# The gate tiles and the first output projection of the merge put between the pieces of a scan

## What is computed

```python
def mixing_sublayer(u_lat, u_ctx, ...):
    a_lat, b_lat, gates_lat = jnp.split(u_lat @ w_in, split_at, axis=-1)
    oa_lat, _ = run_a(a_lat, state_a)              # gated delta rule, "the first mixer"
    ob_lat, _ = run_b(to_col_major(b_lat, rows), state_b)   # RWKV-7 scan, "the second mixer"
    ob_lat = to_row_major(ob_lat, rows)
    g_a, g_b = jnp.split(gates_lat, 2, axis=-1)
    y = jax.nn.sigmoid(g_a) * (oa_lat @ w_o_a) + jax.nn.sigmoid(g_b) * (ob_lat @ w_o_b)
    return y @ w_out
```

## Time and profile before

| | |
|---|---|
| median of 3 runs | 2622.01 us (2617.77 to 2626.14) |
| the profiled execution: its time | 2621.55 us |
| its span | 2619.7 us |
| PE busy | 2470.2 us, 94% |
| DVE, ACT, POOL busy | 1424.4 us (54%), 1186.0 us (45%), 306.8 us (12%) |
| mean granted clock of PE | 0.97 |
| the head of the scan, the scan and the merge | 1881.97 to 2259.1 us |

### The profile page before, as it was taken

The page is one execution under the profiler, slowest core; times in us unless marked ns, Lnnn a source line. Parts: engine busy times, 40 slices in busy tenths (PEclk is TensorE's granted clock), DMA queues, the critical chain, the costliest instruction groups (busy, mean ns, idle before and its releaser), DMA issues.

```text
span 2619.7 us, 52357 instructions
## 1 busy us (share of the span) xinstructions
PE 2470.2 (94%) x23199; PEld 2135.1 (82%) x23199; DVE 1424.4 (54%) x2229; ACT 1186.0 (45%) x1707; POOL 306.8 (12%) x425
## 2 busy tenths in 40 slices
PE   6999999999999999999999989899888889799998
PEld 6999888799999998878899965785477778678786
DVE  4654545466546645443666456445245540278885
ACT  4434466444444444564444355321254421167773
POOL 0100000021101100000311000641133321000000
PEclk8999999999999999999999989889899899899999
DMA  6754522256656644322566411101100004379993
GB/s 217 246 192 167 192 97 104 81 195 233 216 178 213 230 164 171 129 97 101 173 237 222 154 66 46 54 15 57 65 4 4 4 27 141 96 240 365 365 365 126
DMA packets 268884, 396.07 MB, mean 151 GB/s; under 512 B 9320, under 2 KB 172829, under 8 KB 268525
## 3 DMA queue, kind: packets, MB, share of 16 engines
q1 hardware_dynamic: 266921, 389.25, 43.4%
q0 software_dynamic: 1120, 2.17, 0.3%
q10 hardware_dynamic: 612, 1.24, 0.1%
HBM read 391.59 MB, written 1.05 MB: 150 GB/s over the span
## 4 chain that ended last, share of the span: by engine, by line
PE 75%; DVE 8%; issue 5%; DMA 5%; ACT 4%; POOL 2%; SPq 0%; ACTq 0%; DVEq 0%; POOLq 0%
PE ps L282 74%; DMA RB<-in_moe_w_up 5%; DVE gwl L431 2%; POOL H L1415 2%; ACT gwh L422 1%; POOL AR L2535 0%; ACT wh L422 0%; PE ps L1093 0%; DVE wl L431 0%; PE ps L520 0%; DVE AR L1677 0%; ACT AR L2752 0%; DMA RB<-in_ffn_w_gu 0%; ACT AR L2744 0%; DVE AT L1178 0%
## 5 line engine op out<-in xcount | busy, mean ns | idle before, releaser
L431 DVE TENSOR_TENSOR wl<-RB,wh 128x2048 fp32r<-128x2048 f32 (+4 forms) x188 | 412.5, 2197 | 294.5 <-ACT wh L422 293.9
L282 PE MATMUL ps<-H,RB 128*128 128x256 f32 (+1 forms) x1712 | 455.5, 423 | 1.1 <-ACT H L1515 1.1
L422 ACT ACTIVATE wh<-RB 128x2048 fp32r<-128x2048 f32 (+4 forms) x188 | 342.3, 1825 | 236.7 <-PE ps L282 205.3
L282 PEld LDWEIGHTS ps<-H,RB 128*128 128x128 f32 x1712 | 325.5, 193 | 115.1 <-issue 77.4
L282 PE MATMUL ps<-xhf,wl 128*128 128x256 f32 x1408 | 404.4, 287 | 14.0 <-DVE xlf L651 9.3
L282 PE MATMUL ps<-xlf,wh 128*128 128x256 f32 x1408 | 401.0, 285 | 0.0
L282 PE MATMUL ps<-xhf,wh 128*128 128x256 f32 x1408 | 400.8, 285 | 0.0
L282 PE MATMUL ps<-AR 64*64 64x64 f32 (+4 forms) x8296 | 276.1, 242 | 47.2 <-issue 19.7
L282 PEld LDWEIGHTS ps<-AR 64*64 64x64 f32 (+2 forms) x8296 | 241.9, 148 | 80.3 <-issue 51.0
L282 PEld LDWEIGHTS ps<-xhf,wl 128*128 128x128 f32 x1408 | 273.0, 194 | 24.9 <-DVE wl L431 14.8
L282 PEld LDWEIGHTS ps<-xlf,wh 128*128 128x128 f32 x1408 | 273.0, 194 | 0.1
(11 more groups left out here) (425 smaller groups left out, 4155.0 us busy)
## 6 DMA issues: line engine op xcount, KB each, us to landing
RB<-in_ffn_w_gu SPq DMA_DIRECT2D x88, 1024.0 KB, 7.7
RB<-in_w_in SPq DMA_DIRECT2D x25, 2048.0 KB, 7.7
RB<-in_ffn_w_down SPq DMA_DIRECT2D x16, 2048.0 KB, 7.8
RB<-in_w_gate SPq DMA_DIRECT2D x16, 2048.0 KB, 8.2
RB<-in_moe_w_gate SPq DMA_DIRECT2D x32, 1024.0 KB, 7.7
RB<-in_moe_w_up SPq DMA_DIRECT2D x32, 1024.0 KB, 10.2
RB<-in_moe_w_down SPq DMA_DIRECT2D x32, 1024.0 KB, 8.2
RB<-in_ada_w SPq DMA_DIRECT2D x12, 2048.0 KB, 9.9
```

What stands on the lines that cost most here:

```text
L282: return M.matmul(o, lhsT, rhs, start=start, stop=stop, skip_group_check=True)
L422: S.activation(self.pair(h)[0], of(slot_of(*key)), ACT.Copy).then_inc(*did("high", *mark))
L431: V.tensor_tensor(lo, of(slot_of(*key)), hi.bitcast(F32), ALU.subtract).then_inc(*did("low", *mark))
```

## The change

1. The first mixer's 8 output tiles (`merge0`), its 8 gate tiles (`gate0`) and the second mixer's first 4 gate tiles (`gate1`) move into `rwkv_order`, so that all engines meet them between pieces of the scan. In the head stand two output tiles and one gate tile; slots -1 to 3 have one output tile each ahead of `mid` 4 and one gate tile each at their end; slots -1 and 3 have one more gate tile ahead of `mid` 2 (slot 3 with an output tile); slots 4 and 5 end on a `gate1`, and slot 7 has two.
2. POOL's product of a gate tile (now L2960) stands at the same place of POOL's order, and its result goes to other memory (Y0).
3. The meetings ahead of the scan and of the merge go; single waits take their place. The small matrices are copied two tiles earlier in the shift, and the last low-rank sigmoid moves behind the rate's piece of unit 0.
4. `base_b` stands ahead of `prep` 0 in each slot, so that ACT's copies for the inverse come ahead of the decay's sigmoid.
5. The remaining merge starts with the last 4 gate tiles. DVE now reads the second mixer's output tile from PSUM, multiplies and adds it; ACT's copy and POOL's product of it go. The loads of lnx by POOL are issued as soon as the scan's last masks are out. The weights' jobs follow the new order.

The core of the diff:

```diff
-        for i, n in enumerate(("w_o_a_2", "w_o_b_2")):
-            job(("o", i), fill_k(A[n][0], 0, 4, 0, DM), ("merge", i, 7))
+        job(("o", 0), fill_k(A["w_o_a_2"][0], 0, 4, 0, DM), ("merge", 0, 7))
+        for i in range(2):
             for u in range(2):
                 job(("mgate", i, u), fill_k(w2in, 0, KD, G_0 + 1024 * i + 512 * u, 512), ("mgate", i, 4 * u + 3))
+        job(("o", 1), fill_k(A["w_o_b_2"][0], 0, 4, 0, DM), ("merge", 1, 7))
...
-            order = prepared(0, *range(7)) + [(("products", 0, o),) for o in range(2)]
+            def fill(*pieces):
+                return [(piece,) for piece in pieces]
+
+            def gate(c):
+                return [("gate0", c, 0), ("gate0", c, 1)]
+
+            order = prepared(0, 0, 1) + fill(("merge0", 0, 0)) + prepared(0, 2) + fill(*gate(0), ("merge0", 1, 0))
+            order += prepared(0, *range(3, 7)) + [(("products", 0, o),) for o in range(2)]
+            sigmoid = {-1: gate(1), 3: [("merge0", 6, 0)] + gate(6)}
+            middle = {i: [("merge0", i + 3, 0)] for i in range(-1, 3)}
+            middle[3] = [("merge0", 7, 0)]
+            end = {i: gate(i + 3) for i in range(-1, 3)}
+            end[3] = gate(7)
+            end.update({4: [("gate1", 0, 0)], 5: [("gate1", 1, 0)]})
 ...
-                slot = [solve(n, "base_a", 0)] + prepared(p, 0) + [solve(n, "base_b", 0)]
+                slot = [solve(n, "base_a", 0), solve(n, "base_b", 0)] + prepared(p, 0)
                 slot += [solve(n, "mid", 1) + out(i, "out_s", 0), unit(i, "solved", 0), solve(n, "more", 1)]
-                slot += prepared(p, 1)
+                slot += prepared(p, 1) + fill(*sigmoid.get(i, ()))
                 slot += [solve(n, "mid", 2) + unit(i, "state", 0)] + prepared(p, 2) + [solve(n, "more", 2)]
                 slot += [unit(i, "early", 1) + out(i, "out", 0)] + prepared(p, 3)
+                slot += fill(("gate1", 2, 0)) if i == 7 else []
                 slot += [solve(n, "mid", 3) + unit(n, "rows", 0), unit(i, "solved", 1)] + prepared(p, 4)
-                slot += [solve(n, "more", 3)] + prepared(p, 5, 6)
+                slot += [solve(n, "more", 3)] + prepared(p, 5, 6) + fill(*middle.get(i, ()))
+                slot += fill(("gate1", 3, 0)) if i == 7 else []
                 slot += [solve(n, "mid", 4) + out(i, "out_s", 1), solve(n, "more", 4)]
                 slot += [unit(n, "early", 0) + unit(i, "state", 1), solve(n, "mid", 5) + out(i, "out", 1)]
-                slot += [unit(p, "products", 0), unit(p, "products", 1), solve(n, "more", 5)]
+                slot += [unit(p, "products", 0), unit(p, "products", 1), solve(n, "more", 5)] + fill(*end.get(i, ()))
...
+                    if n == 14:
+
+                        AC.wait_ge(*upto("low_rank"))
+                        AC.wait_ge(*at("shift", 13))
+                        S.activation(W2, EARLY[0], ACT.Copy).then_inc(*did("w2"))
...
+                    if n == 13:
+                        DV.wait_ge(*upto("low_rank"))
+                        DV.wait_ge(*at("shift", 13))
+                        V.tensor_copy(A2, EARLY[1])
+                        for i in range(2):
+                            ins = V.tensor_copy(W0[i], EARLY[3][64 * i:64 * i + 1, :])
+                        ins.then_inc(*did("a2"))
...
-            everyone(("moved", 14), ("low_act", 14), ("rv_rows", 3), ("unit_kk", 3))
-
-
-            AC.wait_ge(*upto("low_rank"))
-            S.activation(W2, EARLY[0], ACT.Copy).then_inc(*did("w2"))
-            PO.wait_ge(*upto("low_rank"))
-            P.tensor_copy(G2, EARLY[2]).then_inc(*did("g2"))
-            DV.wait_ge(*upto("low_rank"))
-            V.tensor_copy(A2, EARLY[1])
-            for i in range(2):
-                ins = V.tensor_copy(W0[i], EARLY[3][64 * i:64 * i + 1, :])
-            ins.then_inc(*did("a2"))
-            for mark in (("w2",), ("g2",), ("a2",)):
-                PE.wait_ge(*at(*mark))
...
+                if what == "merge0":
+                    sv = slot_of("o", 0).rearrange("p (k n) -> p k n", k=4)
+                    PE.wait_ge(*landed("o", 0))
+                    PE.wait_ge(*at("o_rows", 1))
+                    ps = bank(("merge", 0, i), ("yb", 0, i), among=kept if i > 1 else (3, 4))
+                    for k in range(4):
+                        ins = mm(ps[:, 0:T], sv[:, k, 128 * i:128 * i + 128], OAT[:, k, :], k == 0, k == 3)
+                    ins.then_inc(*did("merge", 0, i))
+                elif what == "gate0":
+                    sv = slot_of("mgate", 0, i // 4).rearrange("p (k n) -> p k n", k=KD)
+                    if x == 0:
+                        PE.wait_ge(*landed("mgate", 0, i // 4))
+                        bank(("mgate", 0, i), ("mgated", 0, i), among=kept if i else (3, 4))
+                    ps = ps_of("mgate", 0, i)
+                    for k in range(4 * x, 4 * x + 4):
+                        ins = mm(ps[:, 0:T], sv[:, k, 128 * (i % 4):128 * (i % 4) + 128], HA[:, k, :], k == 0, k == KD - 1)
+                    if x:
+                        ins.then_inc(*did("mgate", 0, i))
+                elif what == "gate1":
+                    gate1_pe(i, others)
+                elif what == "prep" and x == 0:
+                    for mark in (("low_act", 12), ("w2",), ("a2",)):
+                        PE.wait_ge(*at(*mark))
...
+                    if what == "merge0":
+                        AC.wait_ge(*at("merge", 0, i))
+                        if i > 1:
+                            AC.wait_ge(*at("weighed_b", 0, i - 2))
+                        S.activation(YBR[i % 2], ps_of("merge", 0, i)[:, 0:T], ACT.Copy).then_inc(*did("yb", 0, i))
+                    elif what == "gate0" and x:
+                        AC.wait_ge(*at("mgate", 0, i))
+                        if i > 1:
+                            AC.wait_ge(*at("weighed_b", 0, i - 2))
+                        S.activation(SGB[i % 2], ps_of("mgate", 0, i)[:, 0:T], ACT.Sigmoid).then_inc(*did("mgated", 0, i))
+                    elif what == "gate1":
+                        gate1_act(i)
...
-                    if what == "prep" and x == 3:
+                    if what == "gate0" and x:
+                        PO.wait_ge(*at("mgated", 0, i))
+                        if i > 3:
+                            PO.wait_ge(*at("kt", 3))
+                        P.tensor_tensor(Y0[i], YBR[i % 2], SGB[i % 2], ALU.mult).then_inc(*did("weighed_b", 0, i))
+                    elif what == "prep" and x == 3:
+                        PO.wait_ge(*at("unit_kk", 3))
                         if i > 1:
...
+                for c in range(4, KD):
+                    gate1_pe(c, every_bank)
+                PE.wait_ge(*at("low_act", 14))
+                PE.wait_ge(*at("g2"))
...
+                    DV.wait_ge(*at("merge", 1, c))
+                    DV.wait_ge(*at("mgated", 1, c))
+                    V.tensor_tensor(SG1[c], ps_of("merge", 1, c)[:, 0:T], SG1[c], ALU.mult).then_inc(*did("yb_v", c))
+                    DV.wait_ge(*at("yb_v", c))
+                    V.tensor_tensor(Y0[c], Y0[c], SG1[c], ALU.add).then_inc(*did("summed", c))
...
+                PO.wait_ge(*at("kt", 7))
+                PO.wait_ge(*at("bon_in", 7))
...
-                for i in range(2):
-                    for c in range(KD):
-                        PO.wait_ge(*at("mgated", i, c))
-                        P.tensor_tensor(YB[i][:, c, :], YB[i][:, c, :], SGB[:, c % 4, :], ALU.mult).then_inc(
-                            *did("weighed_b", i, c))
 
```

More of the change, by code:

```diff
@@ L1452, in block2 @@
             rwkv(area, *tail)
-            merge(area)
         class LastHead:
@@ L2489, in shift_dve @@
                 ins.then_inc(*did("blk"))
-                for n in range(16):
+                for n in range(15):
                     tail_dve(n)
                     i, j = divmod(n, 4)
+                    if n == 13:
[5 more added lines that the diff above has]
+                        ins.then_inc(*did("a2"))
+                        i = 3
                     if 5 <= n < 9:
@@ L2601, in pairs_pe @@
                 u = units[i]
-                if what == "prep" and x == 0:
+                if what == "merge0":
[21 more added lines that the diff above has]
+                        PE.wait_ge(*at(*mark))
                     ps = bank(("w_in", i), ("w_sig", i), among=others)
@@ L2727, in pairs_pe, with gate1_pe, gate1_act @@
                         yield
+            def gate1_pe(c, banks):
+                sv = slot_of("mgate", 1, c // 4).rearrange("p (k n) -> p k n", k=KD)
+                PE.wait_ge(*landed("mgate", 1, c // 4))
+                ps = bank(("mgate", 1, c), ("mgated", 1, c), among=banks)
+                for k in range(KD):
+                    ins = mm(ps[:, 0:T], sv[:, k, 128 * (c % 4):128 * (c % 4) + 128], HA[:, k, :], k == 0, k == KD - 1)
+                ins.then_inc(*did("mgate", 1, c))
+            def gate1_act(c):
+                AC.wait_ge(*at("mgate", 1, c))
```

(14 more changed lines are left out.)

79 lines of the change are left out of this document (33 added, 46 removed).

## The result

The changed kernel takes 2641.16 us (median of 15 runs, 2626.23 to 2651.92), the kernel before, run beside it, 2619.83 us (median of 15, 2610.25 to 2626.14). The ratio is 1.0074 with a 95% interval from 1.0053 to 1.0094 (it isn't the quotient of the two medians, which is 1.0081): **slower by 0.74%, some 19 us**. The forecast was 2626. The result sits at the top of the range, where the second rival stood (the clock falls for long, 2642).

What follows compares the result with a forecast made beforehand. PE holds 75% of the chain of waits; the merge is solid matmuls, the scan has holes. Seven terms were summed to -4.1 us, the clock's +10 made +6, trimmed to +4.5: 2626 us, range 2604 to 2642.

Steps and rivals of the forecast that it cites:

- the second rival: Scan: clock falls last 8 to 10 us, each costing 4.5, so the change is slower: +20.5, 2642 us; chance 0.25.
- The merge: Merge after the scan: output and gate tiles moved out, and the meeting's hole gone, take off 55.7 us, leaving 62.
- The ends of slots: Ends of slots -1 to 3: five gate tiles, each with a 2.55 us PE standstill behind POOL's product and mask: +26.3 us.
- `gate1` at the ends of slots 4 and 5: Two gate tiles without POOL product, 3.47 us each less holes of 1.53 and 0.92: +4.5 us.
- The gates ahead of level 2: Slots -1 and 3: level 2's masks wait behind POOL's product, +5.8 and +9.1, together +14.9 us.
- The head: Between shift and first level of slot -1: PE goes on at full speed, -3.9 us, bounds 0 and -7.
- The output tiles ahead of level 4: Slots -1 to 3: five tiles cost 8.7 us, less half the instruction-fetch holes, 4.3: +3.7 us.
- The clock: PE's half clock behind new standstills, less falls of before at changed places: +10 us, between -6 and +31.
- The length of a fall: PE at half clock for 5 us after each of six new standstills, costing 2.5 us each.
- The trim from +6 to +4.5: Whole sum: halved stretches are also partly bound by other engines, so +6 us was lowered to +4.5.
- the first: Rival: 2.5 us holes don't halve the clock and two falls go, -10.5 us, about 2610; chance 0.22.
- The third: Rival at the inverse: POOL's mask isn't delayed, holes and their falls go, -27 us, 2594; chance 0.07.

Runs made afterwards that it cites:

- run 3: Changed kernel, order kept, with six unread matmuls on PE behind each of the five gate tiles at the ends of slots: 2615.84 us, ratio 0.9997.
- run 6: Changed kernel with only the head's POOL product (gate tile 0) moved behind `bt0`: 2633.76 us, ratio 1.0070.
- run 7: Changed kernel with the output weights' slot freed by slot 3's last gate tile, so two 2 MB loads are issued later: 2641.19 us, ratio 1.0093.
- run 1: Changed kernel with POOL's gate-tile products kept back until after the next masks (in the head, `bt0`): 2599.81 us, ratio 0.9921.
- run 5: Changed kernel with the decay's product put back ahead of the inverse's transpose at each slot's start: 2614.82 us, ratio 0.9988.
- run 4: Changed kernel with three unread matmuls behind each of the five gate tiles at the ends of slots, filling half the hole: 2618.66 us, ratio 1.0014.
- run 9: On run 1's kernel: decay ahead of the transpose in slot -1, output tile 6 ahead of slot 3's rate product, output weights' slot freed later: 2595.23 us, ratio 0.9921.
- run 2: Changed kernel with only the five POOL products at the ends of slots -1 to 3 moved behind their masks: 2611.31 us, ratio 0.9967.

## Why the prediction came out as it did

The range held the result; the likeliest number was 15 us too low, and the mechanism of the second rival, long falls of the clock at the starts of slots, is what happened. That the rival's number, 2642, was met within 1 us is in part luck, as the terms below show.

- **The merge**, -55.7: right, 61.75 us are left for the 62 forecast. (The term's parts as printed add up to 56.3; neighbouring groups overlap a little, and counted by their starts they make 55.8. The seven terms add up to -4.0 and not -4.1.)
- **The ends of slots**, +26.3: the structure was right to 0.3 us. A tile, the hole, the transpose and the decay take 9.67 us at full clock (run 3, 1927.86 to 1937.53) for 9.4 forecast. In the changed kernel they take 12.4, 12.4, 11.1, 10.9 and 12.4 (from the tile's start to the first level); 10.7 us over run 3's are the clock's, ahead of the first level alone.
- **`gate1` at the ends of slots 4 and 5**, +4.5: right. Tile to first level is 6.85 and 5.17 us, before it was 4.79 and 2.44 without a tile: 4.8. No fall follows in this trace; there is no product on POOL, and the standstill is 0.36 us or less.
- **The gates ahead of level 2**, +14.9: right to 0.5. From the tile's start to level 2 are 5.7 us in slot -1 (forecast 5.8) and 9.0 with the output tile in slot 3 (9.1); the waits are 1.96, 1.96 and 1.31.
- **The head**, -3.9: the stated bound came, 0 (26.6 us for 26.5). The products begin 16.3 us after the shift's end, for the 16.0 forecast. The step that failed is that what follows takes "6.6 at full speed": the clock was at half behind the hole of 4.16, the products took 3.47 us for 2.08 and the decay 4.1 for 2.2. From the products to the first level are 10.35 us; at full clock they are 7.14 (run 6).
- **The output tiles ahead of level 4**, +3.7: the issue holes of slots -1 to 3 fell from 8.0 us (8.6 in the prediction) to 4.5, about the half that I took, but one of 4.28 came behind the loads. The step that failed is one that I didn't make: the order of the jobs was in the diff, and its loads were costed at nothing. Of it the time shows nothing for certain (run 7).
- **The clock**, +10: this is the term that was mis-sized. The forecast has 34 us at half clock behind new standstills (5 behind each of six, 4 for the others), takes away 12.8 of before, and counts the head at full clock already in its -3.9. Reckoned the same way, the profiles have 78.5 us at half in the changed kernel and 20.5 outside the head before: 58 more where the forecast has 21, up to 29 us where it has 10. (Against before as it ran, its head at half clock included, the same profiles give the 20.4 of above.) By place, the five ends of slots have 44 us (25 forecast; the stretches above show 7 to 9.8 behind each), the head 10 (5 forecast), and 24 stand elsewhere (4 forecast): 10 behind three of the four waits for DVE's L2893, 10 in the last two slots and 3.4 behind the loads' hole. Run 3 measures 20 us for the five ends.
- **The length of a fall**, 5 us in the forecast: I took it between the 3.2 and the 12.5 of rows 8 and nearer the short one. The row of 3.2 us is followed by dense matmuls of 128x512, the rows of 9.4 and 12.5 by the scan's small ones, and the second rival's text says that the new holes stand ahead of small ones. That this is what makes a fall long isn't shown: behind the hole of 4.28 us the clock was at half for 3.4 us too, amid small matmuls.
- **The trim from +6 to +4.5**, "the halved stretches are also partly bound by other engines": wrong. PE is busy for 9.40 of 9.40 us in the halved stretch at the end of slot -1; there was nothing to hide behind.

Put together for the 25.1 us measured between the shift and the end of out2: -4.1, the clock's 29, the loads' hole of 4.3, 3.0 more of waits for DVE's L2893 (5.2 us, 2.2 before), and 5.4 less of issue holes in slots 4 to 7 (12.4 before, 6.9 now), which no term had. That makes 26.8. The 1.7 us over are not settled; 29 is an upper bound. The second rival had 24.6 for the clock, and neither the 4.3 nor the 3.0 nor the 5.4.

What the prediction said would show it: the clock was 1.00 until 1887 and not until 1889. Slots -1 and 3 are 15.3 and 22.3 us longer (12 to 15 forecast), slots 0 to 2 12.0, 9.1 and 9.9 (6 to 8). The mark set for "slower", a clock below 0.85 in the scan, was too low: 0.89 was enough.

Of the rivals, the first (the clock holds, 2610) fell with the trace, but run 3 shows what it would have been worth: 2616. The third (the products don't hold the inverse, 2594) isn't what the change does; run 1 made it do so and got 2600.

## What to carry to other kernels

When work is put into a gap of a scan, follow what it issues on the other engines: here the tile on PE was paid for as forecast, and a product of 0.72 us in front of a mask on POOL cost 28 us over five places. Price a new standstill of PE as two things, the hole and the clock behind it. Take the second as a range from several rows and, if there are any, several traces: one row is one draw. Count the falls that your sum takes away at the same places, too, so that none is counted twice. If a standstill can't be avoided, give PE something in it, even work that is thrown away, or an operation that was due anyway; both were worth about 20 us here (runs 3 and 5).

## What the runs showed of the hardware

- **The length of a standstill alone doesn't tell whether the clock falls.** At the ends of slots, ahead of the same small matmuls, 1.46 us had no fall in five places (run 4), and 2.75 us had one in 10 of 15: five of five in the changed kernel's trace, three in run 7, two in run 6. One of 1.96 us ahead of level 2 had one in run 5 (running sums 3.42 us) and none in run 3 (1.99). Elsewhere shorter ones had falls of some 3.4 us: 1.44 us in the kernel before (at 1997.83), 1.44, 1.38 and 1.44 in the changed kernel (at 2030.04, 2125.49 and 2159.64), 0.65 and 0.36 at four ends of slots in run 5; and run 6 has a fall in its head with no standstill near. The same instructions differ between executions: 2.9 and 2.6 us ahead of the stretch had falls in before's trace and none in the changed kernel's.
- **The times of one kernel differ with this.** Of the changed kernel's 15 runs, the five with a mean clock of 0.971 to 0.974 took 2626 to 2637 us, the ten with 0.963 to 0.969 took 2632 to 2652. One profiled execution doesn't tell what a standstill costs on average.
- **The fetch of instructions.** In ten traces with loads of weights in the scan, six have an issue hole of 2.98 to 4.55 us while the loads land: five end 7.2 to 8.0 us after the loads were issued, one after 20 with three loads. Away from loads none is over 2.2 us between the shift and the merge. In the changed kernel's hole the DMA engines moved 402 GB/s (stretch 2084.70 to 2088.90). That the fetch waits behind the loads is what this suggests; it was not measured on the queue itself. Moving the loads took the hole out of slot 3 (runs 7 and 9), but runs 1, 2 and 4 have none there without that. Why four of the ten have none is open. By the Trainium skill ("Runtime: NRT & Kernel Launch", section "Instruction fetch mechanics") the sequencer fetches its instructions with a DMA queue of its own. The trace agrees as far as it goes: the changed kernel's page of the profile lists two queues of the kind "instruction", with 185 packets (3.03 MB) and 46 (0.38 MB), though not whose they are.
- **Issue holes differ much between the traces.** Between the shift and the merge they sum to 20.4 us in the kernel before, to 15.7 in the changed kernel (4.3 of it behind the loads), and to 22.0 in run 1, which has no standstill at the ends of slots. That removed standstills come back as issue holes isn't shown by this: runs 6 and 7, which keep the changed kernel's standstills, have 23.8 and 19.4.
